# A two-layer transformer kernel on one core: the first ten expert units in another load order, one modulation unit moved behind the router, squares added before they are summed

## The reference, cut to what matters

```python
def layer(x):                                  # twice
    h = rms_norm(x, norm_mix) @ w_in           # dilated and windowed attention, gates
    x = x + (gates * (branch_a, branch_b)) @ w_out
    h = rms_norm(x, norm_ffn)
    affinity = softmax(h @ w_router)           # 16 experts
    for e in range(16):                        # each expert takes its best 32 tokens
        picked = top 32 tokens of affinity[:, e]
        x[picked] += weight * (silu(h @ gate[e]) * (h @ up[e])) @ down[e]
    return x
```

## Time and profile before

| | |
|---|---|
| median of 3 runs | 2181.93 us (2180.74 to 2183.42) |
| the profiled execution | 2181.32 us, span 2179.5 us, mean TensorE clock 0.978 |
| TensorE busy | 89% of the span |
| DMA | 748.67 MB, 343 GB/s over the span |
| layer 0: head, tiles | about 0 to 268 us, 268 to 711 us |
| layer 1: head, tiles | about 711 to 969 us, 969 to 1443 us |
| second block: mixing, MoE | about 1443 to 1703 us, 1703 to 2180 us |

### The profile page before, as it was taken

The page is one execution under the profiler, slowest core; times in us unless marked ns, Lnnn a source line. Parts: engine busy times, 40 slices in busy tenths (PEclk is TensorE's granted clock), DMA queues, the critical chain, the costliest instruction groups (busy, mean ns, idle before and its releaser), DMA issues.

```text
span 2179.5 us, 32059 instructions
## 1 busy us (share of the span) xinstructions
PE 1937.9 (89%) x14274; PEld 1195.9 (55%) x14274; DVE 640.1 (29%) x980; ACT 546.4 (25%) x837; POOL 0.2 (0%) x4
## 2 busy tenths in 40 slices
PE   8999998787877999998898989879999998888897
PEld 8988832121212898882333434349999744444443
DVE  4476500000000548640241111047657200000001
ACT  4366300000000437630111222033544211011111
POOL 0000000000000000000000000000000000000000
PEclk9999999999999999998999999999999999999999
DMA  9734799999999972679999999974426899999996
GB/s 363 285 126 172 307 408 428 427 428 428 427 428 420 339 258 99 226 302 393 427 423 419 422 423 422 428 280 155 155 78 227 368 427 426 427 425 427 426 427 261
DMA packets 116413, 748.67 MB, mean 343 GB/s; under 512 B 6064, under 2 KB 18736, under 8 KB 79024
## 3 DMA queue, kind: packets, MB, share of 16 engines
q1 hardware_dynamic: 116272, 746.52, 83.8%
HBM read 745.45 MB, written 1.05 MB: 343 GB/s over the span
## 4 chain that ended last, share of the span: by engine, by line
PE 54%; DMA 39%; DVE 4%; ACT 2%; issue 1%; DVEq 0%; SPq 0%; ACTq 0%
PE bank L786 18%; DMA ring<-w_expert_up 13%; DMA ring<-w_expert_down 10%; PE bank L859 10%; PE bank L903 6%; DMA ring<-moe_w_down 6%; DMA ring<-w_expert_gate 5%; PE bank L789 5%; DMA arena<-moe_w_down 4%; PE bank L813 2%; PE bank L890 2%; PE bank L1056 1%; PE bank L1077 1%; PE bank L1177 1%; PE bank L797 1%
## 5 line engine op out<-in xcount | busy, mean ns | idle before, releaser
L859 PE MATMUL bank<-ring,arena 128*32 128x512 f32 (+1 forms) x3264 | 523.1, 511 | 87.8 <-DMA ring<-w_expert_up 48.5
L859 PEld LDWEIGHTS bank<-ring,arena 128*32 128x32 f32 x3264 | 165.4, 109 | 409.8 <-issue 213.1
L903 PE MATMUL bank<-ring,arena 128*32 128x512 f32 x1280 | 283.5, 612 | 59.9 <-DMA ring<-w_expert_down 47.5
L786 PE MATMUL bank<-arena_parts,ring_parts 128*128 128x256 f32 x1296 | 293.8, 283 | 0.0
L786 PEld LDWEIGHTS bank<-arena_parts,ring_parts 128*128 128x128 f32 x1296 | 218.6, 189 | 6.6 <-ACT arena_parts L1667 2.3
L903 PEld LDWEIGHTS bank<-ring,arena 128*32 128x32 f32 x1280 | 67.8, 112 | 255.9 <-issue 155.6
L1667 ACT ACTIVATE arena<-bank 128x512 f32<-128x512 f32 (+1 forms) x142 | 73.8, 544 | 457.3 <-PE bank L874 232.6
L2190 DVE TENSOR_TENSOR arena<-arena,bank 128x512 f32<-128x512 f32 x24 | 15.8, 685 | 564.8 <-PE bank L859 564.8
L786 PE MATMUL bank<-hnT_parts,ring_parts 128*128 128x256 f32 x512 | 144.2, 282 | 0.0
L786 PE MATMUL bank<-ring_parts 128*128 128x256 f32 x688 | 132.3, 284 | 1.8 <-DVE ring_parts L2618 0.9
L859 PE MATMUL bank<-arena 128*32 128x256 f32 (+1 forms) x832 | 109.3, 441 | 8.0 <-DMA arena<-moe_w_up 6.5
(11 more groups left out here) (383 smaller groups left out, 2440.7 us busy)
## 6 DMA issues: line engine op xcount, KB each, us to landing
ring<-w_expert_down SPq DMA_DIRECT2D x64, 2048.0 KB, 25.6
ring<-w_expert_up SPq DMA_DIRECT2D x60, 2048.0 KB, 25.0
ring<-w_expert_gate SPq DMA_DIRECT2D x56, 2048.0 KB, 23.7
ring<-w_in SPq DMA_DIRECT2D x34, 2048.0 KB, 12.0
ring<-moe_w_up SPq DMA_DIRECT2D x24, 2048.0 KB, 28.6
ring<-moe_w_gate SPq DMA_DIRECT2D x20, 2048.0 KB, 34.5
ring<-moe_w_down SPq DMA_DIRECT2D x16, 2048.0 KB, 35.8
arena<-moe_w_down SPq DMA_DIRECT2D x16, 2048.0 KB, 29.9
```

The source lines that it names most:

```text
L786: last = pe.matmul(out[:, n * S:(n + 1) * S], w[:, k, n * P:(n + 1) * P], x[:, k, :], start=first, stop=final)
L859: last = pe.matmul(to[own_rows(half, e)].rearrange("p (q c) -> p q c", c=own), x_slots[:, c, 32 * e:32 * e + 32], w[:, k, half], start=c = ...
L903: last = pe.matmul(banks[4 + e // PAIRS][own_rows(half, e), :].rearrange("p (x d) -> p x d", x=2), hidT[:, e // PAIRS * own + f % own, own ...
```

## The change

Four edits. In this text u3 is unit 3 of tile 0, and slot 3 is ring slot 3.

1. Ada 3 is no longer computed in the head between the projection jobs but after the router, in front of the first token rows; its unit 21 is loaded after the projections' units. The later ada units go to bank 6, the fourth token rows to bank 7.
2. The order and the places of the first ten expert units: u1 and u8 are loaded into the spare slots 8 and 7 in front of unit 23; u2, u3, u4 take slots 0, 1, 2; u9 takes spare slot 6 and is issued between u2 and u3; u5, u6, u7 take slots 3, 4, 5 behind ada 3, 4, 5.
3. The token rows 2, 1 and 3 come after ada 4 and ada 5. In layer 1 the second block's constants are loaded in front of u18, behind a wait for u9, not in front of u14 behind a wait for u7.
4. The squares of chunks 0 to 5 are added on VectorE into chunk 0 (`six_squares`, four more operations), so that the norm needs sums of three chunks, not eight. The same is done in the MoE.

```diff
-FIRST_SLOTS = (9, 8, 7, 0, 1, 2, 3, 6, 4, 5, 9, 8)
+FIRST_SLOTS = (9, 8, 0, 1, 2, 3, 4, 5, 7, 6, 9, 8)
+FIRST_LOADS = (2, 9, 3, 4, 5, 6, 7)
...
-HEAD_ORDER = [0, 18, 1, 19, 2, 20, 3, 21] + list(range(4, 18)) + [22, 23]
+HEAD_ORDER = [0, 18, 1, 19, 2, 20, 3] + list(range(4, 18)) + [21, 22, 23]
...
-ADA_HEAD = 4
-ADA_WITH = ({1: (0,), 2: (1,), 3: (2,), 4: (3,)}, {0: (0,), 1: (1,), 2: (2,), 3: (3,)})
+ADA_HEAD = 3
+ADA_WITH = ({1: (0,), 2: (1,), 3: (2,)}, {0: (0,), 1: (1,), 2: (2,)})
...
                 def router_part(j):
                     chunks_ = [(k, half) for k in (2 * j, 2 * j + 1) for half in range(TH)]
-                    pe.wait_ge(act_done, act_at(f"squares2 {j}", loops))
-                    for k, half in chunks_:
-                        last = pe.matmul(sums_bank[:, half:half + 1], squares_2[:, k, row_of(half)], ones[:, 0:1],
-                                         start=k == 0 and half == 0, stop=k == DC - 1, skip_group_check=True)
                     if j == 3:
+                        pe.wait_ge(dve_done, dve_at("norm2 six", loops))
+                        for k in (0, 6, 7):
+                            if k == 6:
+                                pe.wait_ge(act_done, act_at("squares2 3", loops))
+                            for half in range(TH):
+                                last = pe.matmul(sums_bank[:, half:half + 1], squares_2[:, k, row_of(half)], ones[:, 0:1],
+                                                 start=k == 0 and half == 0, stop=k == DC - 1, skip_group_check=True)
                         last.then_inc(pe_done, pe_p.mark("norm2 sum"))
...
                 router_part(3)
+                ada_unit(ADA_HEAD)
                 token_rows(0)
-                token_rows(2)
...
                 last.then_inc(pe_done, pe_p.mark("aff rows"))
-                token_rows(1)
-                token_rows(3)
-                for n in range(ADA_HEAD, ADA_UNITS):
+                for n in range(ADA_HEAD + 1, ADA_UNITS):
                     ada_unit(n)
+                for j in (2, 1, 3):
+                    token_rows(j)
...
+            def six_squares(step, sq, j, squared):
+
+                if j not in (1, 2):
+                    return
+                dve.wait_ge(act_done, squared)
+                if j == 1:
+                    then(dve.tensor_tensor(sq[:, 0:2, :], sq[:, 0:2, :], sq[:, 2:4, :], ALU.add), step + " four in two")
+                    then(dve.tensor_tensor(sq[:, 0, :], sq[:, 0, :], sq[:, 1, :], ALU.add), step + " four")
+                else:
+                    then(dve.tensor_tensor(sq[:, 4, :], sq[:, 4, :], sq[:, 5, :], ALU.add), step + " two")
+                    dve.tensor_tensor(sq[:, 0, :], sq[:, 0, :], sq[:, 4, :], ALU.add).then_inc(dve_done, dve_p.mark(step + " six"))
...
+                    if i == 23:
+                        sp.wait_ge(pe_done, pe_at(f"o win {WIN_HEADS // 2 - 1}", loops))
+                        load_tile_unit(0, 1)
+                        load_tile_unit(0, 8)
...
-                sp.wait_ge(pe_done, pe_at(f"o win {WIN_HEADS // 2 - 1}", loops))
-                for u in range(1, RING + SPARE):
-                    if u == 7:
+                for u in FIRST_LOADS:
+                    if FIRST_SLOTS[u] == RING:
                         sp.wait_ge(dve_done, dve_at("yb 3", loops))
                     load_tile_unit(0, u)
...
-                    if layer == LAYERS - 1 and unit == ("tile", 0, 14):
+                    if layer == LAYERS - 1 and unit == ("tile", 0, 18):
                         sp.wait_ge(pe_done, pe_at("slot cols", loops))
-                        sp.wait_ge(pe_done, pe_at("tile_0 unit 7", loops))
+                        sp.wait_ge(pe_done, pe_at("tile_0 unit 9", loops))
```

More of the change, by code:

```diff
@@ L1168, in ada_unit @@
                     u = 18 + n
-                    if n % 4 == 0:
-                        ada_banks[n // 4] = take(7, "act", f"ada {min(n + 3, ADA_UNITS - 1)}")
+                    base, end = (0, ADA_HEAD) if n < ADA_HEAD else (ADA_HEAD, ADA_UNITS)
+                    if n == base:
+                        ada_banks[base] = take(6 if n else 7, "act", f"ada {end - 1}")
                     if layer == 0 and n == 0:
@@ L1176, in ada_unit @@
                         for b in range(4):
-                            last = pe.matmul(ada_banks[n // 4][32 * b:32 * b + 32, (n % 4) * P:(n % 4 + 1) * P],
+                            last = pe.matmul(ada_banks[base][32 * b:32 * b + 32, (n - base) * P:(n - base + 1) * P],
                                              c_pairs[:, 2 * k:2 * k + 32], w[:, k, b * P:(b + 1) * P], start=k == 0, stop=k == DC - 1)
@@ L1200, in _ @@
                     pe.wait_ge(consts_loaded, 16)
-                ada_cols("ada 3", to_dve("ada 3 cols"), ada_rows, ADA_HEAD)
+                ada_cols("ada 2", to_dve("ada 2 cols"), ada_rows, ADA_HEAD)
                 pe.wait_ge(dve_done, dve_at("k_win", loops))
@@ L1275, in token_rows @@
                     half, c0 = j // 2, 4 * (j % 2)
-                    out = take((1, 4, 5, 6)[j], "act", f"hn_tok {j}")
+                    out = take((1, 4, 5, 7)[j], "act", f"hn_tok {j}")
                     for c in range(4):
@@ L1563, in router2_part @@
                 chunks_ = [(k, half) for k in (2 * j, 2 * j + 1) for half in range(TH)]
-                pe.wait_ge(act_done, act_at(f"m squares {j}"))
-                for k, half in chunks_:
-                    last = pe.matmul(sums_bank[:, half:half + 1], sq_moe[:, k, row_of(half)], ones[:, 0:1],
-                                     start=k == 0 and half == 0, stop=k == DC - 1, skip_group_check=True)
                 if j == 3:
+                    pe.wait_ge(dve_done, dve_at("m norm six"))
+                    for k in (0, 6, 7):
+                        if k == 6:
+                            pe.wait_ge(act_done, act_at("m squares 3"))
+                        for half in range(TH):
+                            last = pe.matmul(sums_bank[:, half:half + 1], sq_moe[:, k, row_of(half)], ones[:, 0:1],
+                                             start=k == 0 and half == 0, stop=k == DC - 1, skip_group_check=True)
                     last.then_inc(pe_done, pe_p.mark("m norm sum"))
@@ L1840, in ada_copy @@
                     act.activation((ada_rows_late if n0 else ada_rows),
-                                   banks[7][:, 0:(n1 - n0) * P], ACT.Copy).then_inc(act_done, act_p.mark(f"ada {n1 - 1}"))
+                                   banks[6 if n0 else 7][:, 0:(n1 - n0) * P], ACT.Copy).then_inc(act_done, act_p.mark(f"ada {n1 - 1}"))
                 for i, (_, c0, step, _, reader) in enumerate(IN_JOBS):
@@ L1952, in _ @@
                     act.wait_ge(pe_done, pe_at(f"hn_tok {j}", loops))
-                    act.activation(dealt(half, c0), turned_rows(banks[(1, 4, 5, 6)[j]]), ACT.Copy, scale=t_inv[:, half:half + 1]).then_inc(act_done, act_p.mark(f"hn_tok {j}"))
+                    act.activation(dealt(half, c0), turned_rows(banks[(1, 4, 5, 7)[j]]), ACT.Copy, scale=t_inv[:, half:half + 1]).then_inc(act_done, act_p.mark(f"hn_tok {j}"))
                 ada_copy(ADA_HEAD, ADA_UNITS)
@@ L2460, in _ @@
                 kept = 4 * ADA_UNITS * layer
-                ada_cols("ada 3", bank_v(), ada_raw[:, kept:kept + 4 * ADA_HEAD, :])
+                ada_cols("ada 2", bank_v(), ada_raw[:, kept:kept + 4 * ADA_HEAD, :])
                 pairs = WIN_HEADS // 2
@@ L2535, in _ @@
                         low(first + 6 + j)
+                    six_squares("norm2", squares_2, j, act_at(f"squares2 {j}", loops))
                 dve.wait_ge(act_done, act_at("norm2 root", loops))
@@ L2839, in _ @@
                     low2(MIX0 + j + 2)
+                six_squares("m norm", sq_moe, j, act_at(f"m squares {j}"))
             dve.wait_ge(act_done, act_at("m norm root"))
```

## The result

The changed kernel takes 2166.64 us in the median of four runs (2159.85 to 2168.83), beside 2182.68 us for the kernel before (2180.74 to 2185.14, four runs). The ratio is 0.9918, with a 95% interval of 0.9906 to 0.9930; on 2182 us that is 17.9 us, where I had forecast 12.0.

The account below looks back on a forecast made before the run. TensorE bounds the heads, the DMA load stream the tiles. Gains of 3.8 (heads), 2.6 and 3.8 (layer tile stages) and 1.8 (MoE) sum to 12.0 us off 2181.32: 2169 us, range 2165 to 2174.5.

Parts of the forecast that it names:

- the loads' part: Layer tile stages: u13 and u14 no longer late, gaining 2.6 and 3.8 us; MoE stage only shifts by 1.8 us.
- Fewer pauses: Rival, layer tile stages: u8's late issue goes too, both stages reach their upper bounds; 15.1 us gained, 2166.2; chance 0.17.
- Ada 3 out of the head: Both layers' heads: ada 3 leaves TensorE's path, no wait replacing it; 1.88 us twice, 3.8 us gained.
- The squares: Routers: fewer sums bring `mix 3` 1.58 us earlier per layer; MoE gains 1.8 us; VectorE's four additions stay hidden.
- Ada 3 behind the router: Behind `mix 3` in both layers: ada 3 just fits at full clock, affinities at 5.5 us; counted at nothing.
- the half clock: Rival behind `mix 3`: TensorE's clock halves over ada 3, costing 1.7 to 2.8 us per layer; about 2173.5; chance 0.18.
- the first rival: Behind `mix 3`: ada 3 takes 3.76 us at half clock, delaying u5 and token choice; about 2173.5; chance 0.18.
- the rival with 0.18: Behind `mix 3`: TensorE at half clock over ada 3, losing 1.7 to 2.8 us in each layer; about 2173.5.
- Both signs: Behind the router: TensorE's affinity wait becomes VectorE's wait for TensorE; a DMA share under 0.5 behind `mix 3`.
- Slower through late constants: Rival, layer 1 tiles: constants landing four loads later stall TensorE up to 19.6 us; worst 2189; chance 0.03.

Follow-up runs that it names:

- i_moved_back: Changed kernel with 30 one-column products added, so TensorE's program is as long as in the kernel before; 2170.22 us, ratio 0.9937.
- d: Changed kernel with ada 3 put back into the heads, the new unit places kept; run twice: 2166.89 us (0.9917) and 2171.25 us (0.9936).
- second profile: The same changed kernel, nothing altered, timed and profiled once more; 2166.19 us, ratio 0.9917.
- h: Changed kernel with token rows in their old order around the affinities and ada 3, 4, 5 all behind them; 2170.48 us, ratio 0.9949.
- c: Changed kernel with ring slots 0 to 2 given to u3 to u5 and 3 to 5 to u7 to u9; 2173.13 us, ratio 0.9945.
- f: Kernel before with only the new places and order of loads, constants behind u17 included; 2176.01 us, ratio 0.9975.
- b: Changed kernel with the sums of squares as before, eight chunks summed on TensorE; 2173.25 us, ratio 0.9947.
- g: Kernel before with only the squares of six chunks added on VectorE; 2172.94 us, ratio 0.9962.
- j: Kernel before with 34 one-column products added, making TensorE's program 136 instructions longer; 2182.87 us, ratio 0.9992.
- k: Kernel before with the squares change in the MoE's router alone, 40 instructions less; 2181.64 us, ratio 0.9984.

## Why the prediction was right or wrong

**The size was wrong by one missing term; the rest came near as a sum, its terms less so.** Moved back to the old place of the loop, the changed kernel gains 13.7 us (i_moved_back), beside the 12.0 forecast, within its interval of 10.7 to 16.6. The other 4.4 us are the MoE's tile loop, and the step that failed is the last of the loads' part: "In the MoE the load at 1725.22 is released by TensorE, and so the whole stage shifts by the 1.8 us." The stage shifted, and it also became shorter. I took its length as given, because the diff doesn't touch it. The removed sums were priced by their 0.79 us on the path and not as instructions of the program, whose number sets where the loop stands: that place was worth 432.05 less 427.45 us.

The rival "Fewer pauses" named 2166.2, and the measured median is 2166.64. That is luck: its cause was two tile stages at their upper bounds, 3.9 and 5.0 us, and they gave 3.8 and 4.15 in one profile, 2.2 and 2.6 in the other. What brings the time that low is the loop.

**Ada 3 out of the head.** The sign came true (no ada unit in the head's chain). The heads are shorter by 3.0 and 3.5 us in the first profile, 1.5 and 3.6 in the second, around 1.88 with a scatter as large; TensorE's clock fell at other places in them. The term's net worth is 2.1 us by the two runs of d, against 3.8, and between 0 and 4 it stays open.

**The squares.** In layer 0 `mix 3` moved by 4.73 - 2.97 = 1.76 us against the head, where I had 1.58. In the MoE, from the second block's last mixing (1678.33 before, 1663.17 after on the chain) to the first long run of expert products it is 44.65 less 42.92 = 1.73 us, against 1.8. The first load there moved to 1708.32, 16.9 us earlier, where I had named 12, because 15.2 had been gained ahead of this stretch in that execution. VectorE's four additions took 0.68, 0.42, 0.43 and 0.42 us and stayed hidden, as forecast. Without the loop all squares give 3.9 us alone and 2.1 when they are taken back, against about 5.

**Ada 3 behind the router, and the half clock.** "Nothing" was wrong here. The affinities come 5.86 us behind `mix 3` in layer 0 and 7.2 in layer 1, against 5.5 forecast for both. In layer 1 that is the first rival, in part: ada 3 took 2.74 us and the token rows behind it 1.05. In layer 0 the clock stayed at 1.00 in the first profile and fell in the second, where ada 3 took 3.55 us. So the rival with 0.18 is no other case than the forecast: it happens in three of the four layers profiled, and the first gather then comes 15.2 to 15.3 us behind `mix 3`, 13.7 where the clock stayed, and 14.3 before.

Both signs that the forecast named for its being wrong came true in part. TensorE's wait for the affinities (1.09 us in layer 1 before) has become a wait of VectorE for TensorE, and layer 0 of the second profile has a window of share 0.35 behind `mix 3`.

**The loads.** The stretch from the last projections to the tiles' end, with the shift of the squares in it, gave 3.8 and 4.15 us in the first profile, 2.2 and 2.6 in the second, against 2.6 and 3.8 forecast. u13 and u14 are no longer late, as I had counted. What I did not see is how much hangs on the order on TensorE behind the router, which I had counted at nothing: it costs 7.0 us to take back (h), as much as the places, 6.0 us taken back (c) and 5.5 alone (f). In the profiles, places or order undone open a pause of the queue again (share 0.34 from 987 to 993 us in c, 0.19 from 256 to 260 in h). The squares undone open none (in b no 2 us behind `mix 3` have a share under 0.6), and they cost little beyond the loop. Whether the worths overlap or add up lies within the uncertainty.

**Slower through late constants:** nothing of it; layer 1's tiles are 2.1 to 3.3 us shorter.

## What to carry to other kernels

Look at what stands idle with "issue" at a loop's jump back, and at the packets of the instruction queue, before pricing a change: removing or adding instructions anywhere ahead of a loop can switch that cost on or off, and it should be tested by padding alone before the edit is credited with it. In a queue that serves in order, do first what frees the next load's place, even ahead of what the critical chain seems to want. Take an edit's worth from undoing it in the full change and from doing it alone, and take what comes from the code's place out of both first: here the squares would have passed for 6.5 and 8.3 us, of which 4.4 are the loop.

## What the runs showed of the hardware

A loop of 1674 instructions on TensorE was repeated three times without a single fetch in one place, and with nine packets of 16 KB in each repeated pass when it stood 120 instructions later; moved on by another 136, it was free again. TensorE stood still for 4.7 to 6.2 us each time and then began at a granted clock of 0.50 (1814 to 1818 us of before; 16 products in 3.78 us, not 2.05). That time itself is covered, since the loads go on (DMA share 0.99 to 1.02 inside the idle times). What is lost is transfer. Away from the stage's end the weights' queue moves 142.51 MB in 335 us before (1805 to 2140) and 143.45 MB in as long a stretch after (1788 to 2123), 425 and 428 GB/s, which is about 2.2 us. The queue of instructions took 0.5% of the 16 engines' time in 350 us, an estimate of 1.75 us, so it accounts for most of that. Another 1.2 us, by an estimate from 8.08 MB against 8.59 in the last 20 us, are lost at the end, where the DMA engines no longer finish together. The last 8 us, before and after:

```profile
2147.00:2155.00 8.00, 6.83 (x32) 1.54 (x28) 0.00 (x0) 0.60 (x1) 0.00 (x0) 1.00 0.87 369
```

```profile
2125.50:2133.50 8.00, 6.82 (x32) 1.54 (x28) 0.00 (x0) 0.60 (x1) 0.00 (x0) 1.00 1.01 428
```

The share there is 0.87 or 0.88 in b, f and i too, which have the packets, and 1.00 or more in c, g, h and j, which have none. About 1 of the 4.4 us stays open, and so does why k loses 2.5 us by a single stall. Open is also why one place stalls and another doesn't: in the compiled programs the loop's last instruction is number 249 of its block of 256 before and in i (three stalls), 209 in k (one), and 129 after and in j (none). That would fit a fetch ahead that overwrites the loop's start when the end comes near the end of a block, but no run here shows the memory itself.
